# State-space input tables made in turned layout by GpSimd, from rows repeated by DMA

## The chip, the cores and the metric

The kernel runs on one core of one Trainium2 chip. The metric is the device time of one execution in microseconds (us), median of three runs. The engines are named as in the profile: PE (TensorE), PEld (its weight loads), DVE (VectorE), ACT (ScalarE), POOL (GpSimd), SP (the engine that only issues DMAs here).

## What is computed

256 latent and 256 context tokens of width 1024 go through a latent-attention block (MLA, 16 heads), a state-space block (S5) and a third block (two attentions and a gated feed-forward). The change touches tables of the S5 block that depend on its weights alone. Cut to what matters:

```python
lam_dt = lam * dt[:, None]                    # 128 groups x 64 complex poles, two directions
lam_bar = jnp.exp(lam_dt)
b_bar = ((lam_bar - 1.0) / lam)[..., None] * bmat            # [group, pole, 16 inputs]
def step(h, u_chunk):
    bu = jnp.einsum('btgs,gps->btgp', u_chunk, b_bar)
    _, xs = lax.associative_scan(_ssm_combine, (a, bu), axis=1)
    y = jnp.einsum('btgp,gsp->btgs', xs, cmat).real
```

The kernel does the recurrence in blocks of 8 tokens. For that it needs, for each of 32 units (8 sets of groups times 4 quarters q), an input table mb (b_bar times the powers 0 to 7 of lam_bar, with the 8 x 16 inputs on the partitions, 512 KB), an output table mc (c times powers 0 to 8), and for each pair of units the direct 8-token kernel (`kernels`).

## The kernel before

All engines run programs written by hand, in order, with semaphores (`S.up` and `S.at`). In time: the modulation rows and `head_in` (0 to 85 us), 16 gate tiles `n` of the MLA block (to 205), latents and q_rope (to 241), 16 attention heads (to 442), the output product out0 of 16 groups `i` (to 579), S5, the third block. The tables for units 0 to 15 are made during the gate tiles, those for 16 to 31 during out0 and the start of S5 (the last LATE = 4).

For a unit u, DVE (`unit`) makes mc by six tensor_tensor over 576 columns (L2127 to L2138) and mb, with the poles on the partitions, by six over 512 (L2145 to L2154). PE turns mb by eight 128x128 transposes (`unit_turned`, L573, called after gate tile u+2, or out0 group u-14), ACT copies the two banks and stores them to `mb_scratch`, from which SP loads them in S5. For odd u PE then does `kernels(u // 2)`. POOL stores mc (`c_store`) and the direct kernels (`taps_store`, 8 DMAs per pair). DVE's unit u waits for kernels((u-3)//2) and for the store of mc of u-3 (three buffers).

Weights come through a ring of three 2 MB slots, loaded by SP in one order; load i waits until load i-3 was used. `mod_product(l, ct)` (64 short PE instructions) and `mod_turned` make the modulation of layer l; for (0,4) and (0,5) they stand among the gate tiles, and `gate_rows(0)`, which spreads the result into the tile `gtb`, stands just ahead of `unit_turned(15)`. Four of layer 1 stand in the heads given by `MOD_AT`, the last two behind the heads. Next comes `c_turned(2, ql)` for ql 0 and 1 (both in PSUM bank 7, so the second waits for ACT's `c_conjugated` copy, L1400, of the first), then out0.

Of the kernel before, what the change touches and what calls it, by code (L numbers as in the profile page):

```python
# [16 lines left out]
F32 = mybir.dt.float32  # L17
# [23 lines left out]
L = 8  # L41
# [20 lines left out]
MOD_AT = {3: 0, 5: 1, 10: 2, 12: 3}  # L62
# [10 lines left out]
def vector_rows():  # L73
    at, n = {}, 0
    for name, rows in VECTORS.items():
# [21 lines left out]
          "cT_mm": "transposed", "dT_mm": "transposed", "kern_mm": "unit_mm", "mbT_mm": "unit_mm", "st_mm": "s5_mm", "yt_mm": "s5_mm",  # L97
          "yc_mm": "s5_mm", "yT_mm": "s5_mm", "uT_mm": "s5_mm",  "cT": "unit_act", "mbt": "unit_act", "kt": "unit_act", "bbd": "unit_act",
          "xs": "s5_act", "y": "s5_act", "tok": "s5_act", "u_t": "s5_act", "gelu": "s5_act", "mb": "unit_op", "mc": "unit_op", "bbar": "unit_op",
# [7 lines left out]
          "down_x": "unit_op", "down_u1": "unit_act", "down_a5": "unit_act"}  # L107
# [40 lines left out]
def build(nc, a, out, counts, places):  # L148
    with ExitStack() as stack:
# [5 lines left out]
        mb_dram = nc.dram_tensor("mb_scratch", [NU, P, 8 * P], F32).ap()  # L155
        mc_dram = nc.dram_tensor("mc_scratch", [NU, P, 8, P], F32).ap()
# [76 lines left out]
        dtab = take(NU // 2, GS)  # L233
        assert at[0] <= NTT * D
# [7 lines left out]
        mb = take(2, 1024)  # L242
# [3 lines left out]
        assert at[0] <= units_end  # L246
        take, at = carve(chain_at)
# [12 lines left out]
        def mbt_(u):  # L260
            if u >= NU - LATE:
                return sb[:, arena + 2048 + (u % 2) * 1024:arena + 2048 + (u % 2 + 1) * 1024]
            return sb[:, turned_at + (u % 2) * 1024:turned_at + (u % 2 + 1) * 1024] if u < NU // 2 - 2 else hT_flat[:, (u % 2) * 1024:(u % 2 + 1) * 1024]
# [93 lines left out]
        def slot(i, *shape):  # L357
            v = ring[:, i % SLOTS, 0:int(np.prod(shape))]
            names = " ".join("abcd"[:len(shape)])
            return v.rearrange(f"p ({names}) -> p {names}", **{"abcd"[j]: shape[j] for j in range(len(shape))})  # L360
# [6 lines left out]
        loads, load_no = [], {}  # L367

        def load(key, src, shape, freed, parts=None):
            load_no[key] = len(loads)  # L370
            loads.append((src, shape, freed, parts))

# [3 lines left out]
        def mod_load(l, ct):  # L376
            load(("mod", l, ct), ktiles(a["w_mod"][l])[:, :, ct * 512:(ct + 1) * 512], (KD, 512), ("mod_mm", (l, ct)))

        for ct in range(4):
            mod_load(0, ct)  # L380
# [2653 lines left out]
```

## Time and profile before

| | us |
|---|---|
| runs, median of 3 (lowest, highest) | 1571.36 (1570.56, 1573.48) |
| span of the profiled execution | 1571.2 |
| PE busy in it | 1503.4 (96%) |
| DVE busy | 872.9 (56%) |
| POOL busy | 565.2 (36%) |

The span runs from the first to the last instruction of the profiled execution and is the time against which the sum is made; it lies 0.2 us under the median of the runs, and no other time of that execution is listed. Busy shares are averages: PE's is over 90% in nearly all of the 40 slices, DVE's is near 100% only while tables are made.

### The profile page before, as it was taken

Reading aid. Unit: us, or ns where it says so; the run is one execution under the profiler, and the core shown is the slowest. Engines: PE = TensorE matmul, PEld = TensorE weight load, DVE = VectorE, ACT = ScalarE, POOL = GpSimd, SP = SyncE. Lnnn points to the kernel's source line nnn. Section 1 sums busy time; section 2 is a strip of 40 time slices with the busy share of each in tenths; the row PEclk is TensorE's granted clock in tenths of the full one; section 3 lists DMA queues with packets and bytes.
Section 4 is the critical chain, followed back from the end, with each engine's and each line's share of the span. In section 5 each row is a group of like instructions: output and inputs, shape, how many; then the busy total and the mean of one; then the engine's idle time right before and its main releaser. Section 6 shows DMA issues by size and latency. Waiting matters only on the chain.

```text
span 1571.2 us, 25477 instructions
## 1 busy us (share of the span) xinstructions
PE 1503.4 (96%) x10192; PEld 1129.3 (72%) x10192; DVE 872.9 (56%) x1745; ACT 402.3 (26%) x956; POOL 565.2 (36%) x412
## 2 busy tenths in 40 slices
PE   4999989999999999999998999999999999999998
PEld 3455555666655558898877888887788874688887
DVE  5979944554578978378466321243543422265642
ACT  1222243333311222322233011001223550232210
POOL 4013340000002314101002977773496301477774
PEclk9999999999999999999999999999999999999999
DMA  9856771050286646747666455445544133455441
GB/s 332 221 173 194 242 237 45 3 159 14 100 262 228 202 174 180 273 166 287 251 252 260 159 195 182 161 163 185 191 167 146 70 108 107 131 179 164 168 150 68
DMA packets 172605, 272.99 MB, mean 174 GB/s; under 512 B 51405, under 2 KB 85304, under 8 KB 171208
## 3 DMA queue, kind: packets, MB, share of 16 engines
q1 hardware_dynamic: 146096, 201.08, 38.1%
q0 software_dynamic: 16512, 42.49, 8.4%
q10 hardware_dynamic: 9880, 27.78, 4.8%
q8 instruction: 83, 1.36, 0.4%
q14 instruction: 34, 0.28, 0.1%
HBM read 228.26 MB, written 42.99 MB: 173 GB/s over the span
## 4 chain that ended last, share of the span: by engine, by line
PE 88%; DVE 5%; DMA 3%; issue 2%; ACT 2%; POOL 0%; DVEq 0%; ACTq 0%; POOLq 0%
PE bank L499 82%; PE bank L502 6%; DMA memory<-in_w_mod 1%; DMA memory<-mc_scratch 1%; DVE memory L2417 1%; DVE memory L2418 1%; DVE memory L2424 0%; DVE memory L2421 0%; DMA memory<-in_s_log_dt 0%; DVE memory L2574 0%; ACT memory L1514 0%; ACT memory L1386 0%; ACT memory L1738 0%; DVE memory L2445 0%; DVE memory L2444 0%
## 5 line engine op out<-in xcount | busy, mean ns | idle before, releaser
L499 PE MATMUL bank<-memory 128*128 128x256 f32 (+8 forms) x9244 | 1404.7, 355 | 40.4 <-issue 8.5
L499 PEld LDWEIGHTS bank<-memory 128*128 128x128 f32 (+4 forms) x9244 | 1022.3, 166 | 378.1 <-issue 250.1
L2783 POOL DMA_DIRECT2D mc_scratch<-memory x32 | 28.0, 874 | 505.5 <-DVE memory L2138 447.7
L502 PEld LDWEIGHTS bank<-memory 128*128 128x128 f32 (+1 forms) x948 | 109.3, 142 | 59.4 <-issue 33.6
L502 PE MATMUL bank<-memory 128*128 128x128 f32 (+1 forms) x948 | 125.9, 277 | 23.5 <-ACT memory L1358 8.6
L2822 POOL TENSOR_TENSOR memory<-memory 128x1024 f32<-128x1024 f32 (+1 forms) x34 | 80.9, 2378 | 143.5 <-PE bank L499 96.2
L2808 POOL DMA_DIRECT2D memory<-mc_scratch x32 | 17.3, 541 | 189.7 <-PE bank L499 189.7
L2824 POOL TENSOR_TENSOR memory<-memory 128x1024 f32<-128x1024 f32 (+1 forms) x34 | 80.9, 2380 | 2.7
L2789 POOL DMA_DIRECT2D k_scratch<-memory x128 | 76.2, 629 | 14.5 <-ACT memory L1431 14.1
L2827 POOL TENSOR_TENSOR memory<-memory 128x1024 f32<-128x1024 f32 (+1 forms) x34 | 80.0, 2353 | 2.7
L2825 POOL TENSOR_TENSOR memory<-memory 128x1024 f32<-128x1024 f32 (+1 forms) x34 | 80.4, 2366 | 0.0
L2848 POOL TENSOR_TENSOR memory<-memory 128x1024 f32<-128x1024 f32 x11 | 25.9, 2351 | 130.3 <-DMA memory<-in_w_ffn_up 83.5
L2253 DVE TENSOR_REDUCE memory<-bank 128x1 f32<-128x512 f32 (+1 forms) x48 | 30.2, 685 | 61.9 <-PE bank L499 61.9
L2417 DVE TENSOR_TENSOR memory<-memory 128x256 f32<-128x256 f32 x56 | 23.4, 418 | 68.5 <-ACT memory L1608 68.5
L1423 ACT ACTIVATE memory<-bank 128x512 f32<-128x512 f32 x64 | 34.8, 596 | 91.9 <-PE bank L502 91.6
L1514 ACT ACTIVATE memory<-bank,memory 128x512 f32<-128x512 f32 (+1 forms) x64 | 36.3, 579 | 85.5 <-DVE memory L2256 85.5
L2491 DVE TENSOR_TENSOR bank<-bank,memory 128x256 f32<-128x256 f32 x9 | 3.9, 430 | 83.0 <-ACT memory L1707 83.0
L1580 ACT ACTIVATE memory<-bank 128x512 f32<-128x512 f32 x16 | 9.6, 598 | 111.0 <-PE bank L499 111.0
L2127 DVE TENSOR_TENSOR memory<-memory 128x576 f32<-128x576 f32 x32 | 24.1, 754 | 19.2 <-PE bank L499 17.1
L2640 DVE TENSOR_TENSOR memory<-bank,memory 128x256 f32<-128x256 f32 x11 | 4.7, 423 | 49.2 <-PE bank L499 49.2
L1448 ACT ACTIVATE memory<-bank 128x512 f32<-128x512 f32 x16 | 9.6, 598 | 86.3 <-PE bank L499 86.3
L1606 ACT ACTIVATE memory<-bank 128x128 f32<-128x128 f32 x64 | 27.4, 428 | 15.0 <-PE bank L499 15.0
(305 smaller groups left out, 1284.3 us busy)
## 6 DMA issues: line engine op xcount, KB each, us to landing
memory<-in_s_w_glu SPq DMA_DIRECT2D x32, 1024.0 KB, 7.5
memory<-in_w_mod SPq DMA_DIRECT2D x12, 2048.0 KB, 14.1
memory<-in_w_ffn_up SPq DMA_DIRECT2D x22, 1024.0 KB, 6.9
memory<-in_w_in SPq DMA_DIRECT2D x10, 2048.0 KB, 8.0
mc_scratch<-memory POOLq DMA_DIRECT2D x32, 512.0 KB, 4.5
mb_scratch<-memory ACTq DMA_DIRECT2D x32, 512.0 KB, 3.7
memory<-mb_scratch SPq DMA_DIRECT2D x32, 512.0 KB, 7.3
memory<-mc_scratch POOLq DMA_DIRECT2D x32, 512.0 KB, 6.5
```

The source lines that it names most:

```text
L499: return nc.tensor.matmul(o, l, r, start=start, stop=stop, skip_group_check=free)
L502: return nc.tensor.transpose(o, i, ident[0:n, 0:n])
L1423: A(mbt_(u)[:, dr * 512:(dr + 1) * 512], at_bank("mbT", u, dr), ACT.Copy).then_inc(*S.up("mbt", (u, dr)))
L1514: A(o, i, ACT.Exp, bias=st0[:, 24 + 4 * (h % 2) + t:25 + 4 * (h % 2) + t], scale=MLA_SCALE, accum_out=st0[:, 32 + 4 * (h % 2) + t:33 + 4 * ...
L2253: ins = V.tensor_reduce(st0[:, 48 + c + t:49 + c + t + (t == 2)], i, AX, ALU.max)
L2417: tt(tmp(2 * n), at_(v, c + 64 * (i - 1)), r1, ALU.mult).then_inc(*S.up("step", (q, i, 2 * n)))
L2783: pool.dma_start(mc_dram[u], over(mc[:, u % 3, GS:GS + 1], (144, 8), (1, P))).then_inc(*S.up("mc_out%d" % (u % 3), u, by=16))
L2789: pool.dma_start(to, kt[:, kp % 2, (7 - j) * GS:(7 - j) * GS + P]).then_inc(*S.up("k_out%d" % (kp % 2), kp, by=16))
L2822: nc.gpsimd.tensor_tensor(t1, b12, b11, ALU.subtract).then_inc(*S.up("w_sum", (key, 1)))
L2824: nc.gpsimd.tensor_tensor(b12, b22, b12, ALU.subtract).then_inc(*S.up("w_sum", (key, 3)))
L2825: nc.gpsimd.tensor_tensor(t2, b22, t1, ALU.subtract).then_inc(*S.up("w_sum", (key, 2)))
L2827: nc.gpsimd.tensor_tensor(t4, b21, t2, ALU.subtract).then_inc(*S.up("w_sum", (key, 4)))
```

## The change

- **DVE** makes no mb: `unit` keeps its six operations for mc. Once, behind unit 2, `power_rows` computes powers 0 to 7 of all poles, times b's scale, as rows, by a chain of 36 tensor_tensor: four groups of six at 128 columns, one at 256, one at 512.
- **POOL** stores these rows to `pw_scratch`, then per unit loads 128 partitions of raw turned b (8 times the same 16 rows of `bt_scratch`, one DMA) and of powers (each row on 16 partitions, two DMAs), makes mb by four tensor_tensor (two over 1024 columns, two over 512) and stores it to `mb_scratch`. Loads of unit u are issued ahead of the arithmetic of u-1. It starts behind `head_in` and goes through units 0 to 31 without waiting for the other engines' progress, except for the turned b of quarter q.
- **PE** turns only the raw b of each quarter (`b_turned`, eight transposes, four times: one in the head stage, three among the gate tiles) and no unit.
- **ACT** takes over the stores of mc and of the direct kernels, and stores turned b.
- **Places.** POOL's operands lie in ring slot 1 (which the loads leave free from `head_in` to out0) and its results in `gtb`. So `gate_rows(0)` moves behind the attention heads, where ACT first waits for the last two stores of mb, and SP's load of the second out0 weight waits for the last unit. All later modulation products go into the heads (new `MOD_AT`), through slot 0 alone. SP loads the raw b of quarters 2 and 3 among the gate loads, in place of (0,4) and (0,5).

```diff
-MOD_AT = {3: 0, 5: 1, 10: 2, 12: 3}
+MOD_AT = {1: (0, 4), 3: (0, 5), 5: (1, 0), 8: (1, 1), 10: (1, 2), 12: (1, 3), 14: (1, 4), 16: (1, 5)}
...
+        pairs = ring[:, 1, :].rearrange("p (a b n) -> p a b n", a=2, b=2)
+        mixed_b = gtb
...
-            def unit_turned(u):
-                pe.wait_ge(*S.at("mb", u))
-                for dr in range(2):
-                    b = bank(pe, ("mbT", u, dr), [("mbt", (u, dr))], 4 + dr)
-                    for i in range(4):
-                        last = tr(b[:, i * P:(i + 1) * P], mb[:, u % 2, dr * 512 + i * P:dr * 512 + (i + 1) * P])
+            def b_turned(q, i):
+                pe.wait_ge(*S.at("b_load%d" % (q % 2), q))
+                for ql in range(2):
+                    b = bank(pe, ("bT", q, ql), [("bT", (q, ql))], i + ql)
+                    for n in range(4):
...
-                if n >= 2:
-                    unit_turned(n - 2)
+                if n >= 3 and n % 2:
+                    kernels((n - 3) // 2)
+                if n in (6, 10, 12):
+                    b_turned({6: 1, 10: 2, 12: 3}[n], 4)
...
-            mod_product(1, 4)
-            mod_product(1, 5)
-            mod_turned(1, 4)
-            mod_turned(1, 5)
+            gate_rows(0)
             for ql in range(2):
                 c_turned(2, ql, 7)
...
@@ ACT, in unit_stored @@
-                    A(mbt_(u)[:, dr * 512:(dr + 1) * 512], at_bank("mbT", u, dr), ACT.Copy).then_inc(*S.up("mbt", (u, dr)))
-                act.dma_start(mb_dram[u], mbt_(u)).then_inc(*S.up("mbt_out%d" % (u % 2), u, by=16))
+                act.dma_start(mc_dram[u], over(mc[:, u % 3, GS:GS + 1], (144, 8), (1, P))).then_inc(*S.up("mc_out%d" % (u % 3), u, by=16))
...
+                    for j in range(L):
...
+                        act.dma_start(to, kt[:, kp % 2, (7 - j) * GS:(7 - j) * GS + P]).then_inc(*S.up("k_out%d" % (kp % 2), kp, by=16))
@@ ACT, behind the heads @@
+            for u in (NU - 2, NU - 1):
+                act.wait_ge(*S.at("mb_out%d" % (u % 2), u))
+            gate_rows(0)
             for ql in range(2):
                 c_conjugated(2, ql)
@@ DVE, in unit: the six operations of mb @@
-                tt(o[0], w[0], b[0], ALU.mult).then_inc(*S.up("unit_op", (u, 5)))
...
-                tt(o[1], o[1], t[1], ALU.add).then_inc(*S.up("mb", u))
...
+            unit(2)
+            power_rows()
@@ POOL, pair_load and mixed_unit @@
+                pool.dma_start(b, dview(bt_dram, q * P * 8 * P + g8 * GS * 8 * P, (0, 8), (8 * P, GS), (1, 8 * P))).then_inc(*S.up("pair_in%d" % (u % 2), u, by=16))
+                for ql in range(2):
+                    src = dview(pw_dram, (16 * q + 8 * ql + g8) * 4096, (512, 8), (0, GS), (1, 512))
+                    pool.dma_start(w[:, ql * 512:(ql + 1) * 512], src).then_inc(*S.up("pair_in%d" % (u % 2), u, by=16))
...
+                nc.gpsimd.tensor_tensor(both(o), both(b), both(w, 0, 0), ALU.mult).then_inc(*S.up("mix_op", (u, 0)))
...
+                nc.gpsimd.tensor_tensor(both(w), both(b, P, -P), both(w, P, 0), ALU.mult).then_inc(*S.up("mix_op", (u, 1)))
...
+                nc.gpsimd.tensor_tensor(part(o, 0), part(o, 0), part(w, 0), ALU.subtract).then_inc(*S.up("mix_op", (u, 2)))
+                nc.gpsimd.tensor_tensor(part(o, P), part(o, P), part(w, P), ALU.add).then_inc(*S.up("mixed", u))
...
+                pool.dma_start(mb_dram[u], o).then_inc(*S.up("mb_out%d" % (u % 2), u, by=16))
...
+            for u in range(NU + 1):
+                if u < NU:
+                    if u % 8 == 0:
+                        pool.wait_ge(*S.at("bt_out%d" % (u // 8 % 2), u // 8))
+                    pair_load(u)
+                if u:
+                    mixed_unit(u - 1)
@@ SP, in ring_load @@
+                if i == load_no[("out0", 0, 1)]:
+                    sp.wait_ge(*S.at("mixed", NU - 1))
```

The order of PE's instructions among the gate tiles, before. L502 are transposes, the 32x128 rows are `kernels`; the waits name shared semaphores (unit_op is DVE's, unit_act ACT's):

```order
115 L499 MATMUL bank<-memory 128x512 [waits gates,slot1]
116 L499 MATMUL bank<-memory 128x512 x7
117 L502 MATMUL bank<-memory 128x128 [waits unit_act,unit_op]
118 L502 MATMUL bank<-memory 128x128 x3
119 L502 MATMUL bank<-memory 128x128 [waits unit_act]
120 L502 MATMUL bank<-memory 128x128 x3
```

The same place now:

```order
110 L522 MATMUL bank<-memory 128x128 [waits unit_act]
111 L522 MATMUL bank<-memory 128x128 x3
112 L519 MATMUL bank<-memory 128x512 [waits gates,slot2]
113 L519 MATMUL bank<-memory 128x512 x7
114 L519 MATMUL bank<-memory 32x128 [waits dtab,unit_act,unit_op]
115 L519 MATMUL bank<-memory 32x128 x15
```

The eight transposes that followed each tile are gone; the first two rows now are the end of a `b_turned`, which stands there three times in all.

POOL's program now, from the first pair's loads through the first unit to the third pair's loads (drow is the shared semaphore of the pair loads, w_sum that of its own arithmetic):

```order
25 L2814 DMA memory<-bt_scratch 128x1x1024 [waits bmod,ldt_in,head_mm]
26 L2817 DMA memory<-pw_scratch 128x1x512 x2
27 L2814 DMA memory<-bt_scratch 128x1x1024
28 L2817 DMA memory<-pw_scratch 128x1x512 x2
29 L2827 ISA
30 L2827 TENSOR_TENSOR memory<-memory 128x1024 [waits drow]
31 L2829 TENSOR_TENSOR memory<-memory 128x1024 [waits w_sum]
32 L2831 TENSOR_TENSOR memory<-memory 128x4x128 [waits w_sum]
33 L2832 TENSOR_TENSOR memory<-memory 128x4x128
34 L2834 DMA mb_scratch<-memory 128x1024 [waits w_sum]
35 L2814 DMA memory<-bt_scratch 128x1x1024 [waits w_sum]
36 L2817 DMA memory<-pw_scratch 128x1x512 x2
```

Before, POOL had only DMA issues of mc and of the direct kernels in this place. A unit is now four arithmetic instructions and four issues in one queue.

ACT's program behind the heads, now; before, the row of L1410 (then L1400) followed the load of ln_b directly:

```order
231 L1569 DMA memory<-in_ln_g 128x1024
232 L1569 DMA memory<-in_ln_b 128x1024
233 L1387 ACTIVATE memory<-bank 128x512 [waits gtb_mm,mb_out1,mb_out0]
234 L1387 ACTIVATE memory<-bank 128x512 [waits gtb_mm] x3
235 L1410 ACTIVATE memory<-bank 128x2x128 [waits unit_op,transposed]
```

Four copies and the wait for POOL's last two stores have come in front of the copy for which PE's second `c_turned` waits.

## Rows read from the trace of the kernel before

**Rows 1.** The page: span, then busy us, share and instructions by engine.
```profile
span 1571.2 us, 25477 instructions
PE 1503.4 (96%) x10192; PEld 1129.3 (72%) x10192; DVE 872.9 (56%) x1745; ACT 402.3 (26%) x956; POOL 565.2 (36%) x412
```

**Rows 2.** Windows: stretch, busy of PE, PEld, DVE, ACT, POOL; granted clock, DMA share, GB/s.
```profile
88.00:205.00 117.00, 116.16 (x744) 63.24 (x743) 101.68 (x160) 32.06 (x67) 39.43 (x61) 1.00 0.64 210
241.00:442.00 201.00, 196.82 (x1103) 128.82 (x1102) 103.89 (x241) 68.34 (x185) 0.00 (x0) 1.00 0.21 66
449.00:579.00 130.00, 129.16 (x604) 65.92 (x604) 115.25 (x180) 23.99 (x52) 29.18 (x44) 1.00 0.66 213
```

**Rows 3.** Timeline of PE, gate tiles to q_rope: start, us, line, what.
```profile
88.95 1.04 PE L502 MATMUL bank<-memory 128*128 128x128 f32 x8
89.83 7.03 PE L499 MATMUL bank<-memory 128*128 128x512 f32 x16
...
149.91 9.95 PE L499 MATMUL bank<-memory 128*32 128x128 f32 x120
...
208.94 3.81 PE L499 MATMUL bank<-memory 128*128 128x128 f32 x32 [0.35 <-DVE memory L1920]
216.48 1.97 PE L502 MATMUL bank<-memory 128*128 128x128 f32 x8 [3.73 <-DVE memory L2154]
218.38 6.65 PE L499 MATMUL bank<-memory 128*32 128x128 f32 x48
```

**Rows 4.** Timeline of ACT and PE from the last modulation to out0.
```profile
447.57 0.66 ACT L1400 ACTIVATE memory<-bank 128x256 f32<-128x256 f32 x2 [6.11 <-PE bank L502]
448.37 0.63 PE L502 MATMUL bank<-memory 128*128 128x128 f32 x4 [0.84 <-ACT memory L1400]
448.84 20.77 PE L499 MATMUL bank<-memory 128*128 128x512 f32 x48
```

**Rows 5.** Groups by form: POOL's arithmetic and a plain load that it issues.
```profile
L2822 POOL TENSOR_TENSOR memory<-memory 128x1024 f32<-128x1024 f32 x32 | 77.3, 2414 | 136.2 <-PE bank L499 88.9 <-DMA memory<-in_w_in 25.1 <-DVE memory L2467 22.2
L2827 POOL TENSOR_TENSOR memory<-memory 128x768 f32<-128x768 f32 x2 | 3.6, 1810 | 0.2
L2808 POOL DMA_DIRECT2D memory<-mc_scratch x32 | 17.3, 541 | 189.7 <-PE bank L499 189.7
```

**Rows 6.** Timeline of POOL and DVE where both do tensor_tensor on memory.
```profile
862.96 2.80 POOL L2825 TENSOR_TENSOR memory<-memory 128x1024 f32<-128x1024 f32 x1
863.48 2.83 DVE L2463 TENSOR_TENSOR memory<-memory 128x512 f32<-128x512 f32 x1
865.85 2.68 POOL L2827 TENSOR_TENSOR memory<-memory 128x1024 f32<-128x1024 f32 x1
866.24 2.84 DVE L2465 TENSOR_TENSOR memory<-memory 128x512 f32<-128x512 f32 x1
```

**Rows 7.** The power chain's form (42 us): min/median/max ns at 128, 256, 512 columns.
```profile
L2041 DVE TENSOR_TENSOR memory<-memory x6: 284/426/693, 42.1 to 634.3; 128x128 f32<-128x128 f32 x2, 128x256 f32<-128x256 f32 x2, 128x512 f32<-128x512 f32 x2
```

**Rows 8.** DMA issues, from the page: KB each, us to landing.
```profile
mb_scratch<-memory ACTq DMA_DIRECT2D x32, 512.0 KB, 3.7
memory<-mc_scratch POOLq DMA_DIRECT2D x32, 512.0 KB, 6.5
```

**Rows 9.** DVE's operation for mc, gate tiles and out0 together (the page).
```profile
L2127 DVE TENSOR_TENSOR memory<-memory 128x576 f32<-128x576 f32 x32 | 24.1, 754 | 19.2 <-PE bank L499 17.1 <-ACT memory L1400 2.0
```

**Rows 10.** Timeline: a small DVE tensor_scalar on memory beside POOL.
```profile
1217.10 2.34 POOL L2825 TENSOR_TENSOR memory<-memory 128x1024 f32<-128x1024 f32 x1
...
1218.04 1.43 DVE L2585 TENSOR_SCALAR memory<-memory 128x2 f32<-128x2 f32 x1
1219.50 0.37 ACT L1808 ACTIVATE memory<-bank,memory 128x128 f32<-128x128 f32 x1 [4.95 <-DVE memory L2585]
```

**Rows 11.** Groups of DVE by form within 220 to 440 us.
```profile
L2272 DVE COPY memory<-bank 128x512 f32<-128x512 f32 x32 | 20.5, 683 | 7.1 <-PE bank L502 7.1
L2265 DVE TENSOR_SCALAR memory<-memory 128x512 f32<-128x512 f32 x32 | 14.1, 484 | 0.6
L2265 DVE TENSOR_SCALAR memory<-memory 128x256 f32<-128x256 f32 x32 | 9.8, 349 | 0.0
```

**Rows 12.** Timeline: SP issuing half of one raw b load.
```profile
26.85 14.21 SPq L2877 DMA_DIRECT2D memory<-in_s_b_re x4
```

More of the change, by code:

```diff
@@ L233, in build @@
         dtab = take(NU // 2, GS)
+        poles_kept = take(4, P)
+        squared = take(2, P)
         assert at[0] <= NTT * D
@@ L661, in _ @@
             last.then_inc(*S.up("krT_mm"))
-            mod_turned(0, 5, 7)
-            gate_rows(0)
-            unit_turned(15)
+            kernels(7)
             for i in range(2):
@@ L814, in _ @@
                         i = 8 * n + 4 * kh + t
-                        if 2 <= i < 2 + 16 - LATE:
-                            unit_turned(16 + i - 2)
+                        if 3 <= i < 2 + 16 - LATE and i % 2:
+                            kernels(8 + (i - 3) // 2)
                         if i == 7:
@@ L923, in _ @@
                 u_tile(0, jp)
-                if jp < 3:
-                    unit_turned(NU - LATE + jp)
+                if jp == 1:
+                    kernels(NU // 2 - 2)
             gate_tile(20)
-            unit_turned(NU - 1)
+            kernels(NU // 2 - 1)
             u_turned(0)
@@ L2181, in _ @@
                     V.tensor_copy(kr[:, t, 1, :], k_r).then_inc(*S.up("kr", t))
-            for u in range(2, 6):
+            unit(2)
+            power_rows()
+            for u in range(3, 6):
                 unit(u)
@@ L2791, in _ @@
-            for half in range(2):
-                for u in range(16 * half, 16 * half + 16):
-                    c_store(u)
-                    if u % 16 >= 4 and u % 2 == 0:
-                        taps_store((u - 4) // 2)
-                for kp in (8 * half + 6, 8 * half + 7):
-                    taps_store(kp)
+            pool.wait_ge(*S.at("power_rows"))
+            for dr in range(2):
+                e = 1 - 2 * dr
+                to = dview(pw_dram, (7 * 512 if dr == 0 else 0) + dr * 256, (4096, P // 2), (-512 * e, 8), (1, 2 * P))
+                pool.dma_start(to, over(ptab[64 * dr:64 * dr + 64, 0, 0, 0:1], (2 * P, 8), (1, 2 * P))).then_inc(*S.up("pw_out", by=16))
@@ L2799, in mc_load @@
+            pool.wait_ge(*S.at("head_mm", NTT - 1))
+            for dr in range(1):
+                pool.wait_ge(*S.at("pw_out"))
+            for u in range(NU + 1):
[5 more added lines that the diff above has]
+                    mixed_unit(u - 1)
             def mc_load(u0, u1):
```

256 lines of the change are left out of this document (138 added, 118 removed).

## The prediction

> **What bounds the kernel now.** I read the page first [rows 1]: PE is busy for 1503 of 1571 us, so a gain must shorten PE's own program or its waits, and a loss must be a new wait of PE. Then the windows of the three stretches that the change touches [rows 2]: PE is busy for 116 of 117 us among the gate tiles, 197 of 201 in the heads, 129 of 130 in out0. DVE is busy for 102 and 115 us in the two stretches that make tables, and for only 104 of 201 in the heads, where POOL does nothing at all. The timeline of PE shows the tables' share [rows 3]: eight transposes start at 88.95 and the next matmul at 89.83, so one `unit_turned` costs 0.9 us; the two tiles' 16 records of 0.44 us are one gate tile (7 us). The one large wait is for DVE's unit 15, 3.7 us ahead of its transposes at 216.48. At the end of the heads the reader is to see how tight the hand-over is [rows 4]: ACT copies turned c, PE waits 0.8 us for it, turns the rest at 448.37, and out0 starts at 448.84. Whatever stops ACT there stops PE.
>
> **What goes, on PE.** Up to `kernels(7)`, which starts at 218.4 [rows 3]: 16 unit_turned at 0.9 (14.4) less four b_turned at 0.9 (3.6); two products moved into the heads (the 9.95 us at 149.91 hold a tile of 7.0, a `kernels` of about 1.1 by its 40 of the other 104 records, and so a product of 1.9: 3.8 for two); `gate_rows(0)`, moved too (3.8); the waits of 0.35 and 3.73 (4.1). In sum 22.5, so without any new wait kernels(7) would start at 195.9. From there to out0 it is 230.5 us now; the two products and gate_rows come in (7.6), giving 238: out0 at 434 in place of 448.8, 14.8 earlier. In out0 and S5 another 16 unit_turned go (14.4). That is 29.2 us in all, and 1542.0 against the profile's own 1571.2. The profile lies 0.2 us under the median of the runs, so the same sum serves for both.
>
> **POOL's period.** A unit is two tensor_tensor of 1024 columns at 2.41 and two of 512; no row has 512, but 768 take 1.81, so 256 columns are 0.6 and 512 are 1.2 [rows 5]. That is 7.2 us, with four issues at 0.54 (mine are as plain as the load in the row: 128 rows) 2.2, and some 0.1 for each of four waits for its own result: 9.8 us. The loads (6.5 us to landing [rows 8]) are issued a unit ahead and hide behind about 9 us of work. Bounds of this price: 9.6 if the waits cost nothing, 13 if the repeated rows land slower than the unit before is computed (the load's slowest case is not in a row; 1 MB in place of 0.5 in 6.5 us is at most 13).
>
> **POOL's start.** It needs the power rows. DVE comes to unit 2 at about 86 (the row before 88.95 is PE in that unit's tile) and needs 4.5 us for six operations of 0.754 [rows 9]; the chain is 24 operations of 0.284, six of 0.426 and six of 0.693 [rows 7], 13.5 us, some 15 with a wait behind each: done at 105. Two stores, their landing (taken from [rows 8], 3.7 to 6.5), and the first pair's 6.5 us put the first arithmetic at 120.
>
> **The two engines in each other's way.** Nothing of before lets POOL compute while DVE makes tables, so I take the only place where both run tensor_tensor on memory [rows 6]. DVE's operations of 0.69 us take 2.83, and each ends just after a POOL operation ends; POOL's take 2.7 to 2.8 in place of 2.4. They alternate: one DVE operation per POOL operation, 2.9 us for the two. Among the gate tiles this gives POOL a period of 9.8 + 4 x 0.45 = 11.6. DVE gets four operations between POOL's four and some four more during the issues: eight in 11.6 us, or 8.7 us for the six of a unit. PE wants a unit per tile, 7.0 + 1.1/2 = 7.5 us. DVE so loses 1.2 us per unit over units 7 to 15 (11), some 5 at `b_scaled(1)` (three operations, each behind one of POOL's), and had a slack of a few; unit 15 can't start before kernels(6) and then lies between it and kernels(7). I take 16 us of new waits of PE, bounds 3 and 25: kernels(7) at 212. ACT now issues eight stores behind kernels(7), ahead of its q_rope copies: 3 us more, bounds 0 and 5.
>
> The Trainium skill, page "SBUF — State Buffer", section "SBUF: two separate sides", speaks against this change: it says that VectorE and GpSimd share one port pair as an exclusive lock held for the whole instruction, for VectorE operations with two SBUF inputs and for those in a 2-port mode. The trace agrees with the first half, by the 2.83 us of [rows 6]. For the heads it matters whether single-input scalings are caught as well; by the page they are, and a row of this case says so too: a tensor_scalar of two columns takes 1.43 us and ends with POOL's operation (1217.10 + 2.34) [rows 10].
>
> **The heads.** Each head has four scalings on memory, 0.35 and 0.48 us each, between copies and reductions from PSUM [rows 11]. DVE is busy for 6.5 us of a head's 12.6 [rows 2]. If each scaling waits 1.2 us (half an operation of POOL), DVE has 11.3 us of work, still under 12.6; where all four wait a whole operation it has 16. I take 0.5 us per head, 8 in all, bounds 0 and 50. Without any other wait out0 would start at 434 + 16 + 3 + 8 = 461.
>
> **When POOL is done, which decides.** By 212 it has made (212 - 120) / 11.6 = 7.9 units. The other 24.1 fall in the heads, at 9.8 + 0.4 for DVE's scalings: 246 us, so the last unit is done at 458. Then: its store's issue and landing (0.5 + 3.7 [rows 8]), ACT's four gate-row copies (2.4, estimated at twice the 0.33 of a 256-column copy [rows 4], less a little), the copy of turned c (0.7), four transposes (0.5): out0 starts 8 us behind the last unit, at **466 to 467**. This is later than 461 and so it is what counts; the waits of the gate stretch vanish in it. SP's load of the second out0 weight, also held until then, is needed only 27 us into out0 and is hidden. The sum: 1571.2 + (466.6 - 448.8) - 14.4 = 1574.6. Break-even is a last unit at 455; 0.1 us of POOL's period in the heads is 2.4 us of the end.
>
> The rest costs nothing: ACT's stores (ACT busy 32 of 117 us [rows 2]); SP's raw b loads of quarters 2 and 3, 14 us for half of one [rows 12], which come behind gate loads that have more than two tiles of time, though they fill the DMA queues while POOL's first pairs load (2 us on POOL's start, in the upper bound); slot 0 for the products, each loaded in two heads (25 us).
>
> **Rivals.**
> 1. *POOL late, as above*, with a last unit between 450 and 475: 1566 to 1592, at 1575. For it: 32 x 9.8 = 314 us of work even alone, from 120 on, against 314 us until PE would want it at 434. Chance 0.52.
> 2. *The work hides* (the other side): POOL's operations come nearer 9.6 and DVE's idle phases fall where POOL computes, so the last unit is done before 448 and out0 starts with the heads' own end, 434 to 456: 1542 to 1564, likeliest 1558. It decides from a last unit under 455. For it: DVE works in bursts, and only rows with DVE at full load show 2.8 us. Chance 0.27.
> 3. *DVE becomes the bound of the heads*: 16 in place of 12.6 us in half of them, 27 us, out0 at 480 or later: 1588 to 1615. Against it: POOL issues DMAs for a quarter of the time. Chance 0.11.
> 4. *The repeated rows land late*: period 13, last unit at 120 + 32 x 13 = 536: 1650. Against it: the DMA share is 0.21 in the heads [rows 2]. Chance 0.10, most of it with a period nearer 11 and 1600.
>
> **Numbers.** The forecast is rival 1's value, 1575. The range reaches down into rival 2 and up into 3: 1550 to 1600 leaves 0.08 below and 0.11 above; rival 1's own is 1566 to 1592. About 0.2% (3.1 us) is what a measurement of this kernel can tell from no change. Faster: 0.27 of rival 2 and 0.04 of rival 1. Same: 0.13, all of rival 1. Slower: the rest, 0.56.
>
> **What would show it.** In the profile of the changed kernel: POOL's operations of 1024 columns at 2.4 to 2.8 and a unit each 11 to 12 us among the tiles, 10 to 10.5 in the heads; DVE's mc operations at a mean of 1.3 to 1.5 us among the tiles and 0.75 in out0; PE idle ahead of kernels(7) for 10 us and more; ACT's first gate-row copy released by the DMA of mb_scratch at 462; PE idle ahead of the second c_turned. I am wrong if PE goes from the heads into out0 without a wait (then rival 2), or if POOL waits for its pair loads (then rival 4).

## The result and the profile after

| | before | after |
|---|---|---|
| runs, median (lowest, highest), us | 1572.42 (1570.56, 1573.48) | 1647.03 (1645.13, 1648.88) |
| ratio, 95% interval | | 1.0477 [1.0462, 1.0491] |
| span of the profiled execution, us | 1571.2 | 1643.3 |

The changed kernel is 4.8% slower. The forecast of 1575 leaned to slower but lay within 3 us of the kernel before, so it had neither the size nor clearly the sign, and the time lies 47 us above the end of the range. Each timed run is some 1.9 us longer than the span of its own profile. Runs more than 1.5% above the fastest of their kernel are left out of the times below; only two of e8's four are.

The page of the changed kernel: span, busy time by engine, and two of the lines of slices (granted clock and DMA share, in tenths).
```profile
span 1643.3 us, 25009 instructions
PE 1493.5 (91%) x9968; PEld 1113.0 (68%) x9968; DVE 901.1 (55%) x1592; ACT 372.1 (23%) x900; POOL 789.0 (48%) x510
PEclk9996977998999999999999999999999999999999
DMA  9669999888899345374868455454554213344542
```
PE is busy for 10 us less than in [rows 1], where 28 sets of transposes at 0.9 us should have saved 25, and the span grew by 72. So PE waits, most of it in the first third. The timeline of PE there, with kernels(7) at 248.35 and out0 at 525.35:
```profile
112.41 1.13 PE L519 MATMUL bank<-memory 128*32 128x128 f32 x40 [1.46 <-DVE memory L2159]
...
134.71 2.02 PE L519 MATMUL bank<-memory 128*32 128x128 f32 x40 [6.19 <-DVE memory L2163]
...
153.91 1.09 PE L522 MATMUL bank<-memory 128*128 128x128 f32 x4 [16.13 <-ACT memory L1410]
...
224.89 2.02 PE L519 MATMUL bank<-memory 128*32 128x128 f32 x40 [4.37 <-DVE memory L2163]
...
248.35 6.52 PE L519 MATMUL bank<-memory 128*32 128x128 f32 x48 [18.91 <-DVE memory L2231]
269.93 1.08 PE L522 MATMUL bank<-memory 128*128 128x128 f32 x4 [15.06 <-ACT memory L1499]
...
387.25 5.21 PE L519 MATMUL bank<-memory 128*128 128x512 f32 x6 [7.47 <-DMA memory<-in_mla_w_uq]
...
524.89 0.63 PE L522 MATMUL bank<-memory 128*128 128x128 f32 x4 [1.73 <-ACT memory L1410]
525.35 34.90 PE L519 MATMUL bank<-memory 128*128 128x512 f32 x118
```
Kernels(7) is 30.0 us later than in [rows 3], where the sum without new waits had it 22.5 earlier: 52.4 lost, and the waits of PE ahead of it (these five, and 2.5 behind a product) hold 49.5. From there to out0 it is 277.0 us in place of the 238 of the sum: 39.0 lost. From out0 to the end it is 1118.0 against 1122.4: 4.4 gained in place of 14.4.

ACT is released late. Its timeline around the wait of 16.13, ACTq being its queue:
```profile
136.80 0.37 ACT L1436 ACTIVATE memory<-bank 128x240 f32<-128x240 f32 x1 [6.04 <-PE bank L519]
137.20 15.86 ACTq L1440 DMA_DIRECT2D k_scratch<-memory  x8
153.11 0.66 ACT L1410 ACTIVATE memory<-bank 128x256 f32<-128x256 f32 x2 [15.94 <-issue]
```
The eight stores of one pair's direct kernels, the tap stores, which POOL issued in 4.8 us before, hold ACT for 15.86 us, and the copy of turned c for which PE waits stands behind them. The chain that ended last shows a second cost, in the mc stores that moved to ACT's queue as well (start, us, what):
```profile
96.01 13.12 DMA mc_scratch<-memory
109.22 0.76 DVE memory L2152
...
110.98 13.07 DMA mc_scratch<-memory
124.14 2.88 DVE memory L2152
...
187.16 17.67 DMA mc_scratch<-memory
```
DVE's unit waits for the landing of the mc store three units back, 43.9 us of the chain in these three. Among the gate tiles of the kernel before, POOL's mc stores landed in 3.8 to 8.4 us. That the tap stores make them late is not shown: the first of the three was issued ahead of all tap stores, and it and the third stand 0.01 us behind SP's issue of a weight load (96.00 and 187.15). The run e12 comes back to this.

The windows (columns as in [rows 2]) of the gate stretch, the start of the heads and the rest of the heads, and POOL's timeline at its last unit:
```profile
88.00:248.00 160.00, 110.82 (x541) 55.44 (x539) 133.89 (x112) 23.82 (x50) 117.61 (x90) 0.85 0.96 247
248.00:283.00 35.00, 18.51 (x86) 10.56 (x86) 5.08 (x12) 6.95 (x13) 26.54 (x24) 0.70 0.96 270
283.00:525.00 242.00, 222.71 (x1423) 145.75 (x1424) 175.99 (x259) 72.00 (x192) 181.48 (x146) 0.96 0.87 227
```
```profile
489.84 2.34 POOL L2827 TENSOR_TENSOR memory<-memory 128x1024 f32<-128x1024 f32 x1 [2.44 <-DMA memory<-pw_scratch]
...
497.50 0.61 POOL L2834 DMA_DIRECT2D mb_scratch<-memory  x1 [0.30 <-POOL memory L2832]
```
The DMA share is 0.96 where it was 0.64, and 0.87 in heads that had 0.21. POOL is done at 497.5, 39 us later than predicted, and still does not hold out0 here: the heads themselves end only at 523, and PE then waits 1.73 us for ACT. From the page, the groups that answer to [rows 9] and [rows 11], POOL's first operation, and the landings:
```profile
L2827 POOL TENSOR_TENSOR memory<-memory 128x1024 f32<-128x1024 f32 x32 | 76.4, 2389 | 46.0 <-DMA memory<-pw_scratch 46.0
L2152 DVE TENSOR_TENSOR memory<-memory 128x576 f32<-128x576 f32 x32 | 42.1, 1315 | 76.6 <-PE bank L519 50.4
L2294 DVE TENSOR_SCALAR memory<-memory 128x512 f32<-128x512 f32 (+1 forms) x64 | 74.5, 1225 | 0.6
mc_scratch<-memory ACTq DMA_DIRECT2D x32, 512.0 KB, 5.7
memory<-pw_scratch POOLq DMA_DIRECT2D x64, 256.0 KB, 10.9
```
So there are three suspects: the stores (mc and tap) on ACT's queue, POOL's arithmetic beside DVE, and POOL's repeated-row loads, for which it waits 46 us.

### The profile page after: what moved, and what is told of

Same layout as the page of the kernel before. It is cut to its first block, busy times and chain, and to the rows that moved or that the text cites. A ratio compares the mean times of both kernels' runs of the same rounds, so it can differ in the third digit from the quotient of the medians.

```text
span 1643.3 us, 25009 instructions
## 1 busy us (share of the span) xinstructions
PE 1493.5 (91%) x9968; PEld 1113.0 (68%) x9968; DVE 901.1 (55%) x1592; ACT 372.1 (23%) x900; POOL 789.0 (48%) x510
## 3 DMA queue, kind: packets, MB, share of 16 engines
q0 software_dynamic: 28576, 68.68, 15.5%
## 4 chain that ended last, share of the span: by engine, by line
PE 73%; issue 8%; DVE 7%; DMA 6%; ACTq 3%; ACT 2%; POOL 1%; DVEq 0%; POOLq 0%
PE bank L519 70%; PE bank L522 4%; DMA mc_scratch<-memory 3%; ACTq L1440 3%; DMA memory<-in_w_mod 2%; DMA memory<-in_mla_w_uq 1%; DVE memory L2294 1%; DVE memory L2163 1%; DVE memory L2282 1%; DVE memory L2152 1%; POOL memory L2856 1%; DVE memory L2155 1%; DMA memory<-mc_scratch 1%; DVE memory L2285 1%; DVE memory L2156 0%
## 5 line engine op out<-in xcount | busy, mean ns | idle before, releaser
L519 PE MATMUL bank<-memory 128*128 128x256 f32 (+7 forms) x9244 | 1413.8, 357 | 84.6 <-DVE memory L2231 18.9
L519 PEld LDWEIGHTS bank<-memory 128*128 128x128 f32 (+3 forms) x9244 | 1030.4, 166 | 441.5 <-issue 262.9
L522 PE MATMUL bank<-memory 128*128 128x128 f32 (+1 forms) x724 | 99.2, 282 | 61.2 <-ACT memory L1410 23.7
L522 PEld LDWEIGHTS bank<-memory 128*128 128x128 f32 (+1 forms) x724 | 84.4, 144 | 84.5 <-issue 60.4
L2827 POOL TENSOR_TENSOR memory<-memory 128x1024 f32<-128x1024 f32 x32 | 76.4, 2389 | 46.0 <-DMA memory<-pw_scratch 46.0
L2896 POOL TENSOR_TENSOR memory<-memory 128x1024 f32<-128x1024 f32 x11 | 25.9, 2355 | 130.3 <-DMA memory<-in_w_ffn_up 82.2
L2152 DVE TENSOR_TENSOR memory<-memory 128x576 f32<-128x576 f32 x32 | 42.1, 1315 | 76.6 <-PE bank L519 50.4
L2829 POOL TENSOR_TENSOR memory<-memory 128x1024 f32<-128x1024 f32 x32 | 80.1, 2504 | 2.5
L2294 DVE TENSOR_SCALAR memory<-memory 128x512 f32<-128x512 f32 (+1 forms) x64 | 74.5, 1225 | 0.6
L2832 POOL TENSOR_TENSOR memory<-memory 128x512 f32<-128x512 f32 x32 | 47.6, 1487 | 0.0
L2831 POOL TENSOR_TENSOR memory<-memory 128x512 f32<-128x512 f32 x32 | 44.6, 1393 | 2.5
L2155 DVE TENSOR_TENSOR memory<-memory 128x576 f32<-128x576 f32 x32 | 39.0, 1220 | 0.0
## 6 DMA issues: line engine op xcount, KB each, us to landing
memory<-pw_scratch POOLq DMA_DIRECT2D x64, 256.0 KB, 10.9
```

The costliest lines, as they stand in the source:

```text
L519: return nc.tensor.matmul(o, l, r, start=start, stop=stop, skip_group_check=free)
L522: return nc.tensor.transpose(o, i, ident[0:n, 0:n])
L2152: tt(o[0], w[0], c[0], ALU.mult).then_inc(*S.up("unit_op", (u, 0)))
L2155: tt(t[0], w[1], c[1], ALU.mult).then_inc(*S.up("unit_op", (u, 1)))
L2294: ts(o, o, st0[:, 56 + c + t:57 + c + t], None, ALU.mult).then_inc(*S.up("pn", (h, t)))
L2827: nc.gpsimd.tensor_tensor(both(o), both(b), both(w, 0, 0), ALU.mult).then_inc(*S.up("mix_op", (u, 0)))
```

## The experiments

Each kernel was timed in three rounds beside the kernel before (1572.6 to 1572.9 us). Kernels(7) and out0 are starts in its profile; the last column is the span less the start of out0.

| kernel | median, us | ratio, interval | kernels(7) | out0 | out0 to end |
|---|---|---|---|---|---|
| before | 1572.4 | | 218.4 | 448.8 | 1122.4 |
| after | 1647.0 | 1.048 | 248.4 | 525.4 | 1118.0 |
| e1 before, ACT issues stores | 1621.7 | 1.031 [1.029, 1.034] | 238.0 | 482.4 | 1136.8 |
| e2 no arithmetic | 1672.7 | 1.063 [1.062, 1.065] | 269.9 | 550.7 | 1117.3 |
| e3 small loads | 1644.0 | 1.046 [1.043, 1.049] | 256.0 | 527.6 | 1115.8 |
| e4 taps on SP | 1643.5 | 1.045 [1.041, 1.049] | 244.0 | 522.1 | 1118.0 |
| e5 neither: ACT's stores left | 1593.8 | 1.013 [1.011, 1.016] | 215.1 | 467.4 | 1119.4 |
| e6 stores on POOL too | 1566.9 | 0.996 [0.994, 0.997] | 201.7 | 455.2 | 1109.8 |
| e7 arithmetic left | 1635.4 | 1.039 [1.034, 1.044] | 240.0 | 502.2 | 1117.5 |
| e8 taps stored once | 1657.8 | 1.054, no interval | 228.4 | 519.6 | 1141.6 |
| e9 e7 without arithmetic | 1582.2 | 1.006 [1.005, 1.008] | 212.7 | 462.7 | 1117.7 |
| e10 e6, mixing in heads | 1547.2 | 0.984 [0.982, 0.987] | 197.8 | 435.3 | 1106.9 |
| e11 e10, 16 full units | 1595.6 | 1.015 [1.012, 1.018] | 196.5 | 480.9 | 1110.1 |
| e12 before, mc store on ACT | 1581.8 | 1.006 [1.004, 1.007] | 223.6 | 453.9 | 1124.8 |

**e1: one part of the change alone.** In the kernel before, the mc and tap stores go from POOL to ACT.
```diff
                 act.dma_start(mb_dram[u], mbt_(u))...
+                act.wait_ge(*S.at("mc", u))
+                act.dma_start(mc_dram[u], ...)
...
                     A(kt[:, kp % 2, :], at_bank("kern", kp)[:, 0:240], ACT.Copy)...
+                    act.wait_ge(*S.at("kt", kp))
+                    for j in range(L):
+                        act.dma_start(to, kt[:, kp % 2, (7 - j) * GS:(7 - j) * GS + P])...
```


> The kernel before, with one part of the change: ACT issues the mc stores and the eight tap stores of each pair (behind its own copies, as in the changed kernel), POOL issues none. Theory (the stores on ACT's queue hold ACT, and through it PE): ACT needs 6 to 12 us for eight tap stores here too, somewhat less than the 11.6 to 18.3 of the changed kernel since less is moved; PE waits for ACT's copies; 1590 to 1615. Rival A (DVE and POOL in each other's way is the cause) and rival B (the added transfers are the cause): ACT issues eight stores in about 5 us beside idle queues, which hides; 1570 to 1577.

1621.7: 49 us slower, with no table arithmetic on POOL and no added transfer, and 7 us above the expected range. ACT's timeline at the start of the heads, and PE's there:
```profile
240.19 12.75 ACTq L1437 DMA_DIRECT2D k_scratch<-memory  x8
252.99 1.09 ACT L1481 ACTIVATE memory<-bank 128x512 f32<-128x512 f32 x2 [12.83 <-issue]
```
```profile
253.73 1.09 PE L502 MATMUL bank<-memory 128*128 128x128 f32 x4 [10.41 <-ACT memory L1481]
```
Here the queues are less full and eight stores take 5.7 to 12.8 us. The long ones begin beside or 3 us behind SP's issue of weight loads (this one 239.9 and 240.9, one of 12.40 us at 181.40 behind 178.4); the four under 6.3 us have none near. POOL's eight took 4.7 to 5.4 us in all 16 pairs of the kernel before. That stores on ACT's queue cost this much is shown; why an issue is long is not.

**e2 and e3: one of POOL's two burdens removed.** e2 cuts the four tensor_tensor of a unit to one column, e3 the pair loads to 16 KB, both from unit 2 on.
```diff
+                if u >= 2:
+                    both = part = lambda v, c=0, s=P: v[:, c:c + 1]      # e2
...
-                pool.dma_start(b, dview(bt_dram, ..., (1, 8 * P)))
+                pool.dma_start(b[:, 0:2 * n], dview(bt_dram, ..., (1, 2 * n)))   # e3, n = 8
-                    pool.dma_start(w[:, ql * 512:(ql + 1) * 512], src)
+                    pool.dma_start(w[:, ql * 512:ql * 512 + n], src)
```


> The changed kernel with POOL's four tensor_tensor of a unit cut to one column from unit 2 on (the mixed input tables are not computed; all waits, issues and transfers stay). Theory (ACT's stores): eight tap stores still take 10 us or more, kernels(7) starts at 235 or later in place of 248; only the heads get shorter, by DVE's scalings (1.2 back to 0.4 us); 1610 to 1630. Rival A (DVE and POOL in each other's way): kernels(7) at 215 or earlier, 1545 to 1590.

> The changed kernel with POOL's pair loads cut from 1 MB to 16 KB from unit 2 on (the mixed tables are not computed rightly; the arithmetic's sizes, the waits and the number of issues stay). Theory in the form that full DMA queues make ACT's stores slow: eight tap stores take under 8 us, kernels(7) starts at 215 to 225, out0 is held by POOL's last unit or by the heads at 485 to 500: 1600 to 1620. Theory in the form that ACT's stores are slow by themselves, and rival A: no more than 10 us better than the changed kernel, 1637 to 1647.

e2 missed both of its ranges. It is 26 us slower than the changed kernel: POOL, rid of its arithmetic, issues its 1 MB loads as fast as it can, the DMA share is 1.01 from 88 to 248 us, and PE waits 31.5 us for a raw b load and 37.0 for ACT behind its taps. e3 gains 3 us, no more than the runs' spread. That is in the range of its second form (slow by themselves), but for another reason: its tap stores do become short from 162 to 241 us (5.0 to 5.6 us), and PE now waits 43.4 us for DVE, slowed beside POOL. Removing one suspect uncovers the next.

**e4: the taps off ACT.** Those of pairs 0 to 7 are issued by SP between its loads.
```diff
                 if ct == 2:
+                    taps_store(sp, 0)
                     b_load(2)
+                    taps_store(sp, 1)
+                    taps_store(sp, 2)
                 if ct == 3:
                     b_load(3)
+                    taps_store(sp, 3)
+                    taps_store(sp, 4)
             ring(("uq", 0))
+            taps_store(sp, 5)
+            taps_store(sp, 6)
...
+            taps_store(sp, 7)
```


> The changed kernel with the tap stores of pairs 0 to 7 (those of the gate stretch) issued by SP between its loads, not by ACT; those of pairs 8 to 15 stay with ACT. Theory: ACT's copies and mc stores come on time, kernels(7) starts at 212 to 225 in place of 248, and out0 is then held by POOL's last unit, at about 505 in place of 525: 1620 to 1632. Rivals A and B: kernels(7) at 240 or later, 1640 to 1660, with SP's loads later than before.

1643.5, a miss for the theory and in the range of the rivals; the 3 us to the changed kernel are within the spread. SP pays as ACT did. Its timeline has 16 tap stores, and then half a raw b load that takes twice the time of [rows 12]:
```profile
136.14 14.73 SPq L281 DMA_DIRECT2D k_scratch<-memory  x16
...
151.47 28.25 SPq L2936 DMA_DIRECT2D memory<-in_s_b_re  x4
```
PE waits 15.4 us for the b load, 28 us for DVE, and at out0 12.4 us for POOL's last unit.

**e5: both of POOL's burdens removed; ACT's stores left.** The edits of e2 and e3 together.

> The changed kernel with both POOL's arithmetic and its pair loads cut from unit 2 on (one column, 16 KB; the mixed tables are not computed). What is left of the suspects is ACT's stores. Theory (three causes, each enough to hold the gate stretch by itself): the stores alone cost about what they cost in the kernel before (49 us), on top of the 1542 of the sum without waits: 1580 to 1600, with kernels(7) near 235. Rival (the stores hurt only where the added transfers fill the queues): eight tap stores in about 5 us, kernels(7) at 196 to 205, 1545 to 1560.

1593.8, in the theory's range, though kernels(7) starts at 215.1 and not near 235. With e2 and e3 this makes a square, in all of which the stores stay on ACT: arithmetic and loads 1647, arithmetic alone 1644, loads alone 1673, neither 1594. Each of the two is enough to hold the kernel at 1644 or more, and together they add nothing to that. What the loads cost with the stores on POOL, no run shows.

**e6 and e10: nothing of the three left.** Both keep the edits of e2 and e3 and give the stores back to POOL. e6 mixes in between the stores; e10 puts all mixing behind the last tap store of the gate stretch.
```diff
+            for half in range(2):
+                for u in range(16 * half, 16 * half + 16):
+                    if u >= 3:
+                        c_store(u)
+                    if u % 16 >= 4 and u % 2 == 0:
+                        taps_store((u - 4) // 2)
+                for kp in (8 * half + 6, 8 * half + 7):
+                    taps_store(kp)
+                if half == 0:
+                    for u in range(NU + 1):
+                        mixing(u)        # e6: units 0 to 11 inside the loop above
```


> As the run before, and the mc and tap stores are issued by POOL again, as in the kernel before (the mixed tables are not computed). None of the three suspects is left. By the prediction's sum without any new wait this is 1542, with kernels(7) at 196 and out0 at 434. A time over 1555 says that a fourth cause exists (b loads in the gate stretch, SP's order, the products in the heads).

> The run with everything left out (one-column arithmetic, 16 KB loads, mc and tap stores on POOL), but with all of POOL's units behind the last tap stores of the gate stretch, since in that run POOL's tap stores waited behind its units and held ACT for 18.5 us (the mixed tables are not computed). If that order was the only rest, kernels(7) starts at 196 to 198, out0 at 434 to 438, 1542 to 1550: the prediction's sum without a new wait. A time over 1555 says that a fourth cause is left.

e6 gave 1566.9, above the 1555 that it set as its limit: POOL's tap stores came late behind its units, and ACT waited 18.5 us for one ahead of its q_rope copies. With that order mended e10's profile spans 1542.2 us (median 1547.2). PE's timeline of e10 at kernels(7), and the end of it from out0 in the table:
```profile
197.84 4.76 PE L519 MATMUL bank<-memory 128*32 128x128 f32 x48 [3.04 <-DVE memory L2225]
```
Kernels(7), out0 and the span lie 1.9, 1.3 and 0.2 us from the prediction's 195.9, 434 and 1542.0. The match to the tenth is luck: the profile is of the fastest of e10's four runs (1544.1 to 1554.9), and by the medians e10 gains 25.5 of the sum's 29.2 us. PE also still waits 3.0 us for DVE at kernels(7), which the sum had as gone. So what a fourth cause could hold is some 4 us. In sum, the raw b loads, the products in the heads, gate_rows and SP's order cost about what they were given; none was tried by itself.

**e7 and e9: POOL's arithmetic alone.** e7 is e4 with e3's edit, e9 is e7 with e2's as well.

> The changed kernel with the tap stores of pairs 0 to 7 on SP and the pair loads cut to 16 KB from unit 2 on; POOL's arithmetic has its full size (the mixed tables are not computed rightly). What is left is mainly POOL's arithmetic beside DVE. Theory: DVE's units take 11 us for as long as POOL computes, kernels(7) at 230 to 245, 1600 to 1630. Rival (POOL's arithmetic costs what the prediction said, 16 us by kernels(7) and 8 in the heads): kernels(7) at about 212, under 1590.

> The kernel of the run with only POOL's arithmetic left (taps of pairs 0 to 7 on SP, pair loads of 16 KB), and now the arithmetic cut to one column from unit 2 on as well (the mixed tables are not computed). It differs from that run in POOL's arithmetic alone. Theory (while POOL computes, DVE does two operations in POOL's issues and one beside each of POOL's four, so a unit of DVE takes POOL's period of 11.4 us): without it kernels(7) starts at about 202 in place of 240 and the heads are 20 us shorter: 1555 to 1575. Rival (arithmetic costs 16 us in the gate stretch and 8 in the heads, as the prediction had it): 1595 to 1610, some other thing holding kernels(7) at 220 or later.

Kernels(7) of e7 is in the expected range, its median 5 us above; e9 missed its range by 7 us, with kernels(7) at 212.7 and not 202. The arithmetic costs 53 us by the medians and 39 by the profiles (1619.7 and 1580.4; e7's runs spread from 1621.8 to 1641.1), 27 of them ahead of kernels(7). How it does so is seen in e7's timelines of POOL and of DVE over one unit:
```profile
202.77 1.78 POOL L2840 TENSOR_TENSOR memory<-memory 128x512 f32<-128x512 f32 x1
204.84 0.61 POOL L2842 DMA_DIRECT2D mb_scratch<-memory  x1 [0.30 <-POOL memory L2840]
205.45 0.62 POOL L2822 DMA_DIRECT2D memory<-bt_scratch  x1
206.04 1.21 POOL L2825 DMA_DIRECT2D memory<-pw_scratch  x2
207.22 2.40 POOL L2835 TENSOR_TENSOR memory<-memory 128x1024 f32<-128x1024 f32 x1
209.70 2.75 POOL L2837 TENSOR_TENSOR memory<-memory 128x1024 f32<-128x1024 f32 x1
212.52 1.66 POOL L2839 TENSOR_TENSOR memory<-memory 128x512 f32<-128x512 f32 x1
214.14 1.77 POOL L2840 TENSOR_TENSOR memory<-memory 128x512 f32<-128x512 f32 x1
```
```profile
203.34 1.82 DVE L2170 TENSOR_TENSOR memory<-memory 128x576 f32<-128x576 f32 x1
205.08 0.74 DVE L2159 TENSOR_TENSOR memory<-memory 128x576 f32<-128x576 f32 x1
205.75 0.74 DVE L2162 TENSOR_TENSOR memory<-memory 128x576 f32<-128x576 f32 x1
206.42 3.83 DVE L2163 TENSOR_TENSOR memory<-memory 128x576 f32<-128x576 f32 x1
210.17 2.89 DVE L2166 TENSOR_TENSOR memory<-memory 128x576 f32<-128x576 f32 x1
212.98 1.81 DVE L2168 TENSOR_TENSOR memory<-memory 128x576 f32<-128x576 f32 x1
214.72 1.81 DVE L2170 TENSOR_TENSOR memory<-memory 128x576 f32<-128x576 f32 x1
```
Where POOL computes, DVE gets one operation for each of POOL's: it ends 0.6 us behind the end of the one, and the next one of POOL's, begun meanwhile, is longer by 0.4 (1.66 us; 1.26 where DVE is idle). In the 2.7 us in which POOL only issues, DVE gets two in at 0.74 us; the third, begun at 206.42, would be done at 207.2, just as POOL starts, and ends at 210.25. That is six in POOL's period of 11.4 us, just a unit of DVE, and the two engines run in step: PE's kernels come 22.75 us apart (193.84 and 216.59), two units of 11.4. In the trace of the changed kernel the same pattern stands at 135 to 172 us and from 213 on. e9's own rest above e10 is SP's: PE waits 6.4 us for a raw b load and 8.2 for w_uv, loads that stand behind the tap stores on SP's queue.

**e8: the taps stored once.** A complete kernel: one store of 240 columns per pair, spread over the partitions by SP's loads in S5.
```diff
-                    for j in range(L):
-                        act.dma_start(to, kt[:, kp % 2, (7 - j) * GS:(7 - j) * GS + P])...
+                    act.dma_start(k_dram[kp], kt[:, kp % 2, :])...
...
-                sp.dma_start(tt_sb, k_dram[2 * q + hq]...)
+                for j in range(L):
+                    src = dview(k_dram, ... + (7 - j) * GS, (240, GS), (GS * 240, 16), (1, P))
+                    sp.dma_start(tt_sb[j * GS:(j + 1) * GS], src)...
```


> The changed kernel, complete, with the taps stored once (one store of 240 columns per pair in place of eight shifted ones of 128), and spread over the partitions when SP loads them in S5, eight loads of 16 rows in place of one. Theory: ACT issues the store in under 2 us and is on time in the gate stretch, but DVE still waits for POOL and the queues are full: kernels(7) at 230 to 242, 1620 to 1640. If ACT's stores were the whole cause: under 1600.

In the gate stretch it does a little better than expected: the store takes ACT 0.33 to 0.37 us in six of eight pairs, 6.0 at most, and kernels(7) starts at 228.4, 20 us earlier. Yet out0 starts only 6 us earlier. The timelines of POOL, ACT and PE:
```profile
507.93 0.61 POOL L2832 DMA_DIRECT2D mb_scratch<-memory  x1 [0.30 <-POOL memory L2830]
```
```profile
515.98 2.06 ACT L1387 ACTIVATE memory<-bank 128x512 f32<-128x512 f32 x4 [45.99 <-DMA mb_scratch<-memory]
```
```profile
518.75 1.08 PE L522 MATMUL bank<-memory 128*128 128x128 f32 x4 [43.57 <-ACT memory L1410]
```
The heads end at 475 and PE waits 43.6 us for POOL's last unit. This is the mechanism of the prediction's rival 1, hidden in the changed kernel behind heads that were later still. From out0 on e8 loses 24 us against the changed kernel, and so the whole misses its range, at 1652.5 and 1663.0. Its eight loads in place of one in S5 are the only edit there. PE's waits in that part for which the profile names no releaser sum to 21.8 us in place of 4.6, so that the loads are the cause is likely and not shown.

**e11: POOL's arithmetic in the heads alone.** e10 with units 16 to 31 at full size.

> As the run before, with POOL's arithmetic at full size in units 16 to 31, some 150 us of the heads (the mixed tables are not computed rightly). It prices POOL's arithmetic beside the heads alone. Theory: DVE's scalings go from 0.4 to 1.2 us where POOL computes, and PE waits for them: 10 to 14 us more than the run before for the sixteen. The prediction had 0.5 us a head, about 5 for this stretch; then 5 more or fewer.

1595.6. Two costs are in it. The heads' own last matmuls start at 445.83 in place of 427.82, 18.0 us for sixteen units; groups of DVE by form in 280 to 440 us, of e11 and of e10:
```profile
L2288 DVE TENSOR_SCALAR memory<-memory 128x512 f32<-128x512 f32 x22 | 28.1, 1318 | 0.4
```
```profile
L2288 DVE TENSOR_SCALAR memory<-memory 128x512 f32<-128x512 f32 x22 | 10.0, 498 | 0.4
```
And PE waits 29.0 us at out0 for POOL's last unit, late since the full units come last. That wait was not in the expectation, a miss of mine; the 18.0 were above its 10 to 14.

**e12: the mc stores alone on ACT.** In the kernel before, e1's first three lines.

> The kernel before with the mc stores alone on ACT; the tap stores stay on POOL. Theory (it is the eight tap stores of each pair that hold ACT): one mc store is one issue of 0.55 us, 1571 to 1578. Rival (both kinds of stores matter, through ACT's wait for mc): half of the 49 us of the run with both, 1585 or more.

1581.8, 9 us slower, between the two expectations. An issue takes 0.53 us, but PE waits 3.1 us more for DVE ahead of kernels(7), which starts 5.2 us later. DVE waits 10.4 us, in two pieces, for mc stores to land. The timelines of SP, ACT and DVE around the longer one:
```profile
168.92 0.37 SPq L2863 DMA_DIRECT2D memory<-in_w_mod  x1
```
```profile
170.90 0.53 ACTq L1427 DMA_DIRECT2D mc_scratch<-memory  x1
```
```profile
186.00 0.76 DVE L2129 TENSOR_TENSOR memory<-memory 128x576 f32<-128x576 f32 x1 [7.09 <-DMA mc_scratch<-memory]
```
The store lands 15.0 us after its issue, with no tap store on ACT's queue. Of the 16 mc stores of this stretch the three slowest (10.9, 11.7 and 15.0 us) are those issued 2 us behind a weight load of SP's (97.78, 131.44, 168.92). So the late landings of mc stores come with their own move to ACT's queue, beside SP's weight loads. The other 40 of e1's 49 us come with the tap stores.

## Why the prediction was right and wrong

- **The sum without new waits: right to about 4 us.** 1542.0 against e10's 1542.2 by the profile, 25.5 us of 29.2 by the medians (for a timed run the sum is some 1.9 us higher, which the prediction overlooked); out0 to the end gains 15.5 against 14.4. What goes on PE, what moves into the heads, and the raw loads were sized correctly in sum.
- **"ACT's stores" at nothing, and 3 us behind kernels(7): the step that failed first.** The prediction put "ACT's stores" under what costs nothing and argued from ACT's busy time (32 of 117 us). In these kernels it is not busy time that holds a queue in order but how long one issue takes and what stands behind it, and no row of an issue of such stores on ACT stood behind the price. On ACT they cost 49 us in the kernel before (e1: 9 by the mc stores, as e12 shows, and 40 more with the tap stores), and 45 between the profiles of e5 and e10, whose POOL units also stand in another order. In the changed kernel they are PE's waits of 16.1 and 15.1, the landings of 13 to 18 us that DVE waits for, and probably the 10 us missing from out0 to the end (e5 has 1119.4 there as well, e10 1106.9).
- **The gate stretch's wait for DVE, 16 us (bounds 3 and 25): right mechanism, mis-sized.** The prediction gave DVE four operations during POOL's issues, so eight in a period and 8.7 us for a unit. It gets two, and a unit takes 11.4. Over the nine units 7 to 15 that is 9 x (11.4 - 7.5) = 35, an estimate; e7 less e9 shows 27.
- **POOL's start and period: start right, period low.** First arithmetic at 124.1 (120 predicted). Among the tiles a unit takes 12.1 us (stores 133.01 to 242.20, nine units) against 11.6, in the heads 11.7 (252.69 to 497.50, 21 units) against 10.2. The arithmetic is as priced; the differences sum to 35 us, and POOL's waits for pw_scratch loads, 46.0 us less the first unit's 9.3, are 37. The loads land in 10.9 us where [rows 8] had 6.5, with the DMA share at 0.87 in the heads and not at the 0.21 of [rows 2]. Rival 4 so was partly true.
- **The heads, 8 us (bounds 0 and 50): too low by half.** e7 less e9 gives 17 (262.2 and 250.0 us to out0, less their waits for w_uv of 3.3 and 8.2), e11 18 for sixteen units. With ACT's 15.1 and the uq weight's 7.5, which SP issued late behind the modulation weights, that makes 39.6, against the 39.0 us lost there; since the 17 are from other runs, so close a match is partly chance.
- **Out0 8 us behind POOL's last unit: not what held it here.** In e8, where it did, out0 came 12 us behind the store's issue; the landing took 8.0 of them (507.93 to 515.98) where issue and landing had been given 4.2. With a last unit at 497 to 510 this floor alone would have given 1627 to 1640 (12 us more to out0, then 1118): rival 1 at another size.
- **The Trainium skill's rule**, page "SBUF — State Buffer", section "SBUF: two separate sides", that whichever starts first has the shared port pair for its whole instruction, agrees with e7's rows in that the engines take turns by whole operations. In these rows what DVE gets done is a count of POOL's operations, not a share of time; by that count the estimate above is 35 us in place of 16. One thing does not fit: nine times in e7, and at 206.42 in the rows shown, a DVE operation that began 0.4 to 0.8 us ahead of POOL's first ended 0.6 us behind it, and not before it. Why is open.

The granted clock adds to this, which the prediction had not counted: 0.85 from 88 to 248 us and 0.70 in the 35 us after, in place of 1.00 in e10, where PE hardly idles. Behind the idle time of 6.19 us the 40 records of kernels take 2.02 us, with 0.50 granted (1.2 GHz), in place of 1.13 at 112.41, with 1.00 (2.4 GHz). Over the whole kernel PE is busy for 1493.5 us with the instructions that take 1476.4 in e10; how much of these 17 us lengthens the kernel was not separated from the waits.

**No complete version is faster than the kernel before.** e10, which does not compute the tables, shows what the layout is worth if POOL's work were free: 25 us by the medians, 29 by the profiles. Half of the units on POOL, in the heads only, would cost the 18.0 of e11 for half of those 29; this is an estimate from those rows, without the waits for POOL's last unit, and it was not tried.

## What to carry to other kernels

When a DMA issue moves from one engine's queue to another's, price it by that queue's own issues of such a store while big loads are under way, and list every instruction and landing behind it. Where POOL and DVE both work on memory, count operations: DVE gets one for each of POOL's and what fits whole into POOL's pauses. If several suspects are each enough to hold the path, removing one shows nothing or the reverse; remove all, match the sum, and add them back one at a time.

## What the runs showed of the hardware

- The same eight stores of 128 x 128 took 4.7 to 5.0 us when POOL issued them, in 77 of 80 cases of five traces (5.4 to 5.9 in the others), 5.0 to 18.3 when ACT did, in one case of e2 32.9, and 4.9 to 14.1 when SP did. The long ones come where the DMA share is near 1 or beside weight loads just issued by SP; why an issue is then long was not settled. One store of 240 columns took 0.33 to 0.37 us in six of eight cases, 6.0 at most.
- mc stores on ACT's queue landed 10.9 to 15.0 us after an issue 2 us behind a weight load of SP's (e12), and 4.1 to 8.2 us otherwise.
- DVE's tensor_scalar on memory with one input is caught as well: 1.32 us in place of 0.50 beside POOL's tensor_tensor (e11 and e10).
- POOL without arithmetic was worse than with it (1672.7 against 1647.0), with the DMA share at 1.01 in place of 0.96 from 88 to 248 us; that its earlier transfers do it is how I read this.
